# Identity products on TensorE between the expert products of a diffusion-transformer layer

## The reference

```python
q = (hc @ wq).reshape(PEER_CHUNK, PEER_HEADS, 2, D_HALF)      # 128 tokens, 8 heads
s = jnp.einsum('chsd,hskd->chsk', q, subkeys)
vals, idx = lax.top_k(s, PEER_TOPK)                            # 16 of 128 keys, twice
...
sc, pos = lax.top_k(cand..., PEER_TOPK)                        # 16 of 256 pairs
ex = jnp.take_along_axis(cand_idx..., pos, axis=-1)            # 16 experts per token and head
g = jax.nn.softmax(sc, axis=-1)
act = jax.nn.gelu(jnp.einsum('chkd,cd->chk', u[ex], hc))
return jnp.einsum('chk,chkd->cd', g * act, v[ex])
```

## Time and profile before

| | |
|---|---|
| median of 3 runs | 2249.9 us (2246.74 to 2259.41) |
| the profiled execution: its own time | 2254.92 us |
| its span, first to last instruction | 2253.3 us |
| mean granted clock of TensorE | 0.923 |
| busy: TensorE, VectorE, ScalarE, GpSimd | 1853.2, 1372.0, 637.1, 1190.6 us |
| gathers | 1024 of 512 KB |

### The profile page before, as it was taken

How to read it: one execution, slowest core, us unless ns; L and a number is a source line. 1 busy time by engine, 2 the same in 40 slices (tenths; PEclk the granted TensorE clock), 3 DMA queues, 4 the chain that set the end, 5 groups by cost and what they waited for, 6 DMA issues and landing times.

```text
span 2253.3 us, 21588 instructions
## 1 busy us (share of the span) xinstructions
PE 1853.2 (82%) x6378; PEld 994.1 (44%) x6378; DVE 1372.0 (61%) x3520; ACT 637.1 (28%) x1510; POOL 1190.6 (53%) x1543
## 2 busy tenths in 40 slices
PE   7999899999998798989979877676777676767767
PEld 2554357999985643444434332222222222322222
DVE  1189853777875685755547565655656555566553
ACT  3155412455433242222222221122211122122111
POOL 2100003455453555666656666666766666666665
PEclk9999999999999898999989988888988888999889
DMA  6344355444457789999999999999999999999997
GB/s 234 121 153 155 107 161 138 120 116 134 118 143 239 270 313 347 371 389 390 391 373 350 372 365 363 362 365 382 369 365 363 370 372 360 377 357 379 359 365 291
DMA packets 295261, 657.34 MB, mean 292 GB/s; under 512 B 71568, under 2 KB 141296, under 8 KB 295152
## 3 DMA queue, kind: packets, MB, share of 16 engines
q0 software_dynamic: 150336, 552.67, 64.5%
q1 hardware_dynamic: 144816, 103.36, 15.7%
HBM read 633.40 MB, written 22.54 MB: 291 GB/s over the span
## 4 chain that ended last, share of the span: by engine, by line
PE 31%; issue 14%; POOL 11%; DMA 6%; another core or an unknown queue 5%; DVE 3%; ACT 2%; POOLq 0%; ACTq 0%; DVEq 0%
PE banks L1974 22%; POOL arena L1575 10%; DMA arena<-in_peer_v_dram,arena 5%; PE banks L1995 3%; PE banks L553 2%; PE banks L1473 2%; DVE arena L1914 1%; DMA arena<-in_peer_u_dram,arena 1%; ACT arena L1628 0%; PE banks L2003 0%; ACT L1650 0%; ACT L1725 0%; PE banks L2045 0%; POOL arena L1610 0%
## 5 line engine op out<-in xcount | busy, mean ns | idle before, releaser
L1974 PE MATMUL banks<-arena 128*128 128x512 f32 x1984 | 992.4, 650 | 317.6 <-issue 250.8
L1974 PEld LDWEIGHTS banks<-arena 128*128 128x128 f32 x1984 | 391.3, 205 | 905.1 <-issue 854.1
L1914 DVE CUSTOM_DVE_ANT_0 arena<-arena,banks 128x1024 f32<-128x1024 f32 x512 | 614.2, 1216 | 221.0 <-DMA arena<-in_peer_u_dram,arena 168.1
L1575 POOL DMA_INDIRECT arena<-in_peer_v_dram,arena x504 | 475.2, 943 | 346.7 <-issue 129.4
L1575 POOL DMA_INDIRECT arena<-in_peer_u_dram,arena x512 | 483.5, 944 | 189.6 <-issue 146.8
L1628 ACT ACTIVATE arena<-arena 128x128 f32<-128x128 f32 x496 | 182.2, 397 | 886.7 <-remote 338.4
L2560 PE MATMUL banks<-arena 128*128 128x512 f32 x224 | 109.1, 593 | 0.8 <-ACT arena L2230 0.7
L2645 PE MATMUL banks<-arena 128*128 128x512 f32 x192 | 85.6, 605 | 5.8 <-issue 5.8
L760 POOL TENSOR_TENSOR arena<-arena 128x512 f32<-128x512 f32 x48 | 52.4, 1127 | 65.0 <-issue 48.8
L1995 PE MATMUL banks<-arena 128*128 128x384 f32 x256 | 85.8, 486 | 0.8 <-ACT arena L1334 0.8
L1931 DVE TENSOR_TENSOR arena<-arena 128x16 f32<-128x16 f32 x32 | 5.7, 177 | 101.5 <-issue 70.9
(11 more groups left out here) (338 smaller groups left out, 2536.6 us busy)
## 6 DMA issues: line engine op xcount, KB each, us to landing
arena<-in_w_mod_dram SPq DMA_DIRECT2D x18, 1024.0 KB, 6.8
arena<-in_peer_wq_dram SPq DMA_DIRECT2D x16, 1024.0 KB, 10.8
arena<-in_w_in_dram SPq DMA_DIRECT2D x27, 512.0 KB, 4.2
arena<-kr_scratch SPq DMA_DIRECT2D x96, 128.0 KB, 3.6
arena<-in_peer_u_dram,arena POOLq DMA_INDIRECT x512
arena<-in_peer_v_dram,arena POOLq DMA_INDIRECT x512
arena<-in_w_mod_dram SPq DMA_DIRECT2D x3, 2048.0 KB, 12.2
bk_scratch<-arena POOLq DMA_DIRECT2D x8, 768.0 KB, 3.6
```

The costliest lines, as they stand in the source:

```text
L1575: pool.indirect_dma_start(ring[:, j % RING, :], None, table, bass.IndirectOffsetOnAxis(ap=idx[:, hi % 4, j:j + 1].bitcast(U32), axis=0)).t ...
L1914: nc.vector.tensor_tensor_reduce(u_ring[:, j % RING, :], u_ring[:, j % RING, :], h2cur, 1.0, 0.0, ALU.mult, ALU.add, acts[:, h % 2, j:j + ...
L1974: m = nc.tensor.matmul(PO[h][:, :], diag[:, j % 4], v_ring[:, j % RING, 512 * h:512 * h + 512], start=hp == 0 and j == 0, stop=hp == HEADS ...
```

## The change

From turn 11 on, TensorE multiplies the identity with itself into bank 0, whose content nobody reads. Behind each expert product of the heads 11 to 30 it makes two such products, after the semaphore has been raised; and ahead of the products of each of the heads 10 to 30, twenty. None of them raises a semaphore. Ahead of the first twenty it waits once until ScalarE has copied the last of the late scores out of the bank. At the first head of a tile the twenty come behind the wait for `final_vector`.

```diff
     def tensor6(pe):
+        def keep_clock(n):
+
+            for _ in range(n):
+                nc.tensor.matmul(psum[0][:, 0:P], ident, ident, start=True, stop=True)
+
         def experts(g, hp, js):
...
                 m.then_inc(experts_added, 1)
+                if g > HEADS + 2:
+                    keep_clock(2)
...
                     experts(g - 1, (h - 1) % HEADS, range(13, NSL))
                 else:
+                    if g == HEADS + 3:
+                        pe.wait_ge(late_scores_moved, 2 * HEADS)
+                    keep_clock(20)
                     experts(g - 1, (h - 1) % HEADS, range(NSL))
```

## The result

The changed kernel takes 2306.03 us (median of 4 runs, 2304.35 to 2312.3), the kernel before 2253.27 (4 runs): a ratio of 1.0263, with an interval of 1.0224 to 1.0301. I had forecast 2258 and a range up to 2274, that is 8 us more than the 2249.9 of before and at most 24; it is 53 us slower.

The account below looks back on a forecast made before the run. It took the expert stage to be bound by its gathers, with late news of finished products causing GpSimd's waits. Twenty heads (3 us) plus tile starts (5 us) gave +8 us on 2249.9, so 2258 us, range 2232 to 2274.

Parts of the forecast that it names:

- What bounds the kernel: Expert stage: gathers bound it; GpSimd waits 6 us a head because news of finished products, not the products, comes late.
- The price of a product: Filler on TensorE: 0.24 us a product, 12.5 us a head, 1060 products, 254 us more TensorE work.
- The warm row: Profile row behind the filler's price: 32 records back to back in 3.84 us, 0.12 us each at full clock.
- My bound of doubling: At 1.2 GHz filler was estimated at double; cold throughout at the tile starts, the twenty take 9.6 us.
- What hides it: Expert heads: pairs lie in TensorE's idle time; the twenty's 4.8 us fit the about 6 us to spare before a head.
- TensorE keeps gaining: In a backlog a product with its pair takes 2.2 us, under the 2.48 us GpSimd needs for two gathers.
- Heads 4 to 7 as the nearest row: Late query products there add 12.3 us a head at 46.0 against 45.7 us; so 0 to 6 us, 3 taken.
- The tile starts: First heads of tiles 2 and 3: the twenty lack cover behind the accumulator's wait; 5 us, bounds 0 and 17.
- The rivals: Alternatives for the whole kernel: faster by a kept clock (0.26), slower by delayed bursts (0.30), or +0 to +7 us, within the forecast.
- The clock did rise: Rival: filler keeps TensorE's clock up, so cycles grow from 22 to 25 gathers; -15 to -20 us, 2232 us, chance 0.26.
- The slowed burst: Rival: filler costs products in the 15 us after a release, so cycles shrink; +20 to +25 us, 2272 us, chance 0.30.
- Busy time: Sign to check in the profile after: TensorE busy near 2100 us with 1060 filler products.

Follow-up runs that it names:

- the twenty alone: The changed kernel without the pairs behind expert products, against the kernel before: 2284.21 us against 2247.29 on a slower chip (1.0167), 0.9996 on a faster one.
- The wide filler: The changed kernel with five 512-column products for the twenty and one of 256 for the pair: 2260.31 us against 2247.29 for the kernel before, slower chip.
- chip 2: A chip of the slower kind on which both kernels were run again unchanged: the change 2305.68 us, the kernel before 2244.62.
- its halves: The changed kernel with only the pairs, or only the twenty, against the kernel before: 1.0056 and 1.0167 on slower chips, 1.0002 and 0.9996 on faster.
- half the bytes: The changed kernel with gathers of heads 11 to 30 fetching 512 of 1024 elements: 2310.05 us on a slower chip, 2077.1 on a faster one.

## Why the prediction was wrong

- *What bounds the kernel.* Right for the kernel before. That the news of a product comes late is in the trace; what I took from it, that TensorE's own stream was well, was not. The changed kernel lets ScalarE and GpSimd go just when TensorE's slow stretch ends, which suggests that the late news and the stalls are one thing. That is argued from the times of one head, not shown.
- *The price of a product, the step that failed.* "0.12 us each at the full clock; a product is 0.24 us ... Twenty ahead of a head: 4.8 us." On the slower kind of chip the twenty took 11.9 us, with the pair before them 12.3: about 1.2 for the first nine records, 3.7 until single starts end, 6.3 for 31 records at 0.205 us behind them because the clock had fallen, and 1.1 for the last record and a gap. The warm row, at 724 us, stems from the token mixer; the first gather starts at 740.2. On the faster kind the sum was right: 44 records in 4.91 us, and no loss. The pairs were sized well: 0.44 us against 0.48, and 2.17 us from product to product against 2.2. My bound of doubling, the cold 9.6 us, I used at the tile starts alone.
- *What hides it.* It failed by the same number. "So about 6 us are to spare and 4.8 fit, narrowly": 11.9 don't, and the twenty alone cost 37 us. With 4.8 us a head needs 16 x 2.17 + 4.8 = 39.5 us of TensorE, with 12.3 it needs 46.6, and the pace before was 45.7. So "TensorE keeps gaining" held within a head and failed over a whole one. The chip of the faster kind shows the same sum the other way: 39.5 us of work, 41.7 us a head, no loss.
- *Heads 4 to 7 as the nearest row.* Their late queries are 384 columns wide, 16 records in 5.33 us, where twenty products are 40 records. The wide filler, made like them, lost 0.77%; the change lost 2.6. I compared array time, and the number of instructions was what differed.
- *The tile starts.* The sign and the place were right: all forty records behind the accumulator's wait, at 0.16 us, 6.4 us of them; the V gather waited 5.72 us where I had 3 to 4. In the traces the two tile starts with the head behind each take 12 us more than before, and 27 on chip 2, where I had 5 and at most 17; most of it is in the head behind, which no longer catches up. No run sets them apart from the rest.
- *The rivals.* The clock did rise, to 0.92 in the stage, and an expert record went from 663 to 609 ns: 64 records a head, 3.5 us of them, where the filler adds 15 x 0.44 + 12.3 = 18.9. A warm engine bought nothing because the filler itself stands ahead of the products. The slowed burst had the sign and the direction (GpSimd's waits rose to 9.0 us a head, 928 less 610 x 1.24 over 19.1 heads), but under half of the price, +20 to +25 us where +53 came, and another place: it lost products one by one at 2.2 us, the trace lost the whole front of a head.
- *Busy time*, forecast near 2100 us, was 2055; the stalls are idle time, so a busy line can't show them.

What stays open: what makes single instructions start 0.7 to 2.8 us apart, on some chips and not on others. It isn't the bytes moved, nor the columns. A pause of 0.1 us behind each gather leaves the late news as it was; whether GpSimd's issuing has a part in either is not shown. The Trainium skill (NOTIFIC — the notification-queue block, Overflow: three behaviours, one of which stalls the engine) describes a queue of records which, when it is full, can stall the engine that makes them; no run here tests it.

## What to carry to other kernels

Price filler by a row of the stage where it will run, in number of instructions, not in columns: on the slower chips twenty 128-column products and a pair took 12.3 us here, five of 512 columns and one of 256, as many columns, 4.72. Add up each engine's work for a whole period with the filler in it and compare with the pace, here 46.6 against 45.7 us. Compare too what stands in one piece ahead of a product that others wait for with what can be spared there: the twenty alone, 40 us a head, fitted the pace and still cost 37 us. Where short instructions that wait for nothing stand 0.7 us or more apart in the trace before, expect added ones to do the same; and as another chip may not have it at all (1.0006 here against 1.0267), compare on one chip.

## What the runs showed of the hardware

- The same kernel takes 2115 to 2117 us on three chips and 2245 to 2247 on three others. In its two traces of the slower time gathers go at 368 and 370 GB/s and the clock is 0.87 and 0.88 (windows of 1293 to 2221 us). No trace of the kernel before is from a chip of the first kind; the change, its halves and the one with ScalarE's copies have 404 to 406 GB/s and 0.99 there.
- On the slower kind, short instructions in the gather stage start 0.7, 1.4, 2.1 or 2.8 us apart in stretches of some microseconds: 75.9 us of it in front of the filler of 19 heads, 7.0 with wide products, 79.6 at half the bytes.
- Products of 32 columns follow each other no faster than those of 128: 0.11 us a record with the clock at 1.00, 0.213 at 0.50.
- On a chip without stalls, 1920 memsets of 0.06 us on VectorE, which is busy 67% of the stage without them, with a wait for the dot product in front of every six, cost 12 us, 960 copies on ScalarE none.
